# A latent-attention prologue with its key places one iteration sooner, its row roots earlier on GpSimd, and idle transposes ahead of its first products

## The reference, cut to what matters

```python
def mla_project(h, w_in, q_a_g, kv_a_g, w_uq, w_ukv, qk_g_q, qk_g_k, pos):
    c_q, c_kv, k_pe = jnp.split(h @ w_in, ODD_SPLIT, axis=-1)          # 512 | 256 | 64 columns
    q = to_heads(rms_norm(c_q, q_a_g) @ w_uq, MLA_HEADS)
    kv = to_heads(rms_norm(c_kv, kv_a_g) @ w_ukv, MLA_HEADS)
    ...
    q = rms_norm(q, qk_g_q); k = rms_norm(k, qk_g_k)                    # then rotary positions
```

## Time and profile before

| what | value |
|---|---|
| median of 3 runs | 3112.95 us (3111.66 to 3117.14) |
| the profiled execution's own time | 3118.48 us |
| its span in the trace | 3116.7 us |
| mean granted PE clock | 0.958 of full |
| PE busy / DVE busy / ACT busy / POOL busy | 91% / 68% / 50% / 23% of the span |
| prologue of the latent attention | about 1638.6 to 1812 us of the span |
| main part of the latent attention | about 1812 to 2375 us |

### The profile page before, as it was taken

The page is one execution under the profiler, slowest core; times in us unless marked ns, Lnnn a source line. Parts: engine busy times, 40 slices in busy tenths (PEclk is TensorE's granted clock), DMA queues, the critical chain, the costliest instruction groups (busy, mean ns, idle before and its releaser), DMA issues. The chain is left out here.

```text
span 3116.7 us, 47472 instructions
## 1 busy us (share of the span) xinstructions
PE 2840.2 (91%) x16808; PEld 2280.3 (73%) x16808; DVE 2119.9 (68%) x2536; ACT 1558.8 (50%) x2199; POOL 719.8 (23%) x1243
## 2 busy tenths in 40 slices
PE   6999998869489999999996879999998949999998
PEld 3766676758377777777766768888887838888887
DVE  3576762944666776777655457776765479999997
ACT  2312112532155555555544356766674227777775
POOL 0000000820011211211204665565620001111111
PEclk8999998989789999999998999999999969999999
DMA  6357734444548878878862000000013369999995
GB/s 226 117 208 241 250 115 172 147 177 144 209 180 296 298 292 295 298 294 293 298 234 86 18 9 16 25 16 20 8 66 112 129 268 381 400 396 384 400 400 187
DMA packets 129837, 631.41 MB, mean 203 GB/s; under 512 B 14913, under 2 KB 29377, under 8 KB 70946
## 3 DMA queue, kind: packets, MB, share of 16 engines
q1 hardware_dynamic: 117410, 591.86, 50.0%
q0 software_dynamic: 12288, 37.75, 4.8%
HBM read 563.40 MB, written 66.16 MB: 202 GB/s over the span
## 5 line engine op out<-in xcount | busy, mean ns | idle before, releaser
L1823 DVE TENSOR_TENSOR ex_wlo<-ring,ex_whi 128x2048 fp32r<-128x2048 f32 x384 | 877.4, 2290 | 213.2 <-ACT ex_whi L1752 208.5
L1752 ACT CAST ex_whi<-ring 128x2048 fp32r<-128x2048 f32 x384 | 727.5, 1904 | 295.1 <-PE psum L1717 210.8
L1717 PE MATMUL psum<-ex_whi,ex_xh 128*128 128x512 f32 x1024 | 403.8, 394 | 0.0
L1717 PE MATMUL psum<-ex_whi,ex_xl 128*128 128x512 f32 x1024 | 399.4, 390 | 0.0
L1717 PE MATMUL psum<-ex_wlo,ex_xh 128*128 128x512 f32 x1024 | 398.7, 389 | 0.0
L469 PE MATMUL psum<-fr_whi,fr_hh 128*128 128x512 f32 x560 | 223.9, 401 | 12.8 <-DVE fr_hl L653 11.4
L1717 PEld LDWEIGHTS psum<-ex_whi,ex_xh 128*128 128x128 f32 x1024 | 192.2, 188 | 45.1 <-issue 6.6
L1717 PEld LDWEIGHTS psum<-ex_whi,ex_xl 128*128 128x128 f32 x1024 | 192.2, 188 | 40.8
L1717 PEld LDWEIGHTS psum<-ex_wlo,ex_xh 128*128 128x128 f32 x1024 | 192.4, 188 | 38.6
L469 PE MATMUL psum<-fr_wlo,fr_hh 128*128 128x512 f32 x560 | 218.1, 391 | 0.7 <-DVE fr_wlo L659 0.7
L469 PE MATMUL psum<-fr_whi,fr_hl 128*128 128x512 f32 x560 | 218.2, 391 | 0.0
(11 more groups left out here) (305 smaller groups left out, 6021.7 us busy)
## 6 DMA issues: line engine op xcount, KB each, us to landing
ring<-in_moe_w SPq DMA_DIRECT2D x384, 1024.0 KB, 8.5
fr_raw<-in_mod_w SPq DMA_DIRECT2D x40, 1024.0 KB, 5.8
rec_d<-fr_work SPq DMA_DIRECT2D x72, 256.0 KB, 6.1
fr_raw<-in_ev_w_in SPq DMA_DIRECT2D x14, 1024.0 KB, 5.8
ring<-rec_d SPq DMA_DIRECT2D x10, 1024.0 KB, 15.3
h_d<-ring SPq DMA_DIRECT2D x18, 512.0 KB, 3.0
fr_arena<-in_mod_w SPq DMA_DIRECT2D x8, 1024.0 KB, 11.9
ring<-mod_d SPq DMA_DIRECT2D x15, 512.0 KB, 7.4
```

What stands on the lines that cost most here:

```text
L1717: last = nc.tensor.matmul(g.psum[:, 2 + i % 2, :], x[:, 4 * b + k, :], w[n][:, k, :], start=(b == 0 and k == 0 and first == 0), stop=(b == ...
L1752: nc.scalar.copy(whi[m % RING][:, :, :], slot(i)[:, 4 * b:4 * b + 4, :]).then_inc(hi_set, 1)
L1823: nc.vector.tensor_tensor(wlo[n][:, :, :], slot(i)[:, 4 * b:4 * b + 4, :], whi[n][:, :, :].bitcast(F32), ALU.subtract).then_inc(lo_set, 1)
```

## The change

In `Heads`, `first[p]` becomes a pair: the query place of tile `ORDER[p-2]` and the key place of tile `ORDER[p-1]`, either of which may be None. So the key place of a tile comes one iteration sooner, after the query place, while the sequence of place numbers stays as it was. On POOL `root(1)` comes ahead of the three `low_w`, and in the loop `root(p+3)` after `latent_root(p)` stands in for `root(p+2)` at the head. On ACT `square(1)` follows `square(0)` directly, ahead of the casts of blocks 2 to 7, and `high_up(0)`/`low_up(0)` (the key weight's high and low part) move from iteration 1 to iteration 0. On PE, 36 transposes of the identity into PSUM bank 7 stand ahead of `turn_h(0)`, behind a wait for the first weight cast, and 12 behind it; nobody reads them.

```diff
-        self.first = [[s for s, step in enumerate(self.steps) if p >= 2 and step[1:] == (0, self.ORDER[p - 2])]
-                      for p in range(NT + 2)]
+        at = {step[:1] + step[2:]: s for s, step in enumerate(self.steps) if step[1] == 0}
+        self.first = [(at.get(("q", self.ORDER[p - 2])) if p >= 2 else None,
+                       at.get(("k", self.ORDER[p - 1])) if 1 <= p <= NT else None) for p in range(NT + 2)]
...
 # TensorE
+                pe.wait_ge(wh_set, 1)
+                turn_idle(nc, g, 7, 36)
                 turn_h(0)
+                turn_idle(nc, g, 7, 12)
                 for p in range(NT + 2):
-                    places = hd.first[p]
+                    queries, keys = hd.first[p]
...
-                    if places:
-                        place(places[0])
+                    if queries is not None:
+                        place(queries)
                     if latent:
                         down(p, 3, QL, KVL + ROPE, latkv_out, kv_sum)
                     if p == 0:
                         turn_h(1)
-                    if len(places) > 1:
-                        place(places[1])
+                    if keys is not None:
+                        place(keys)
...
 # ScalarE
                 square(0)
+                square(1)
                 for k in range(2, 5):
                     high_w(k)
                 high_h(0)
                 for k in range(5, KD):
                     high_w(k)
-                square(1)
...
                     if p == 0:
                         high_h(1)
-                    if len(places) > 1:
-                        place(places[1])
-                    if p == 1:
                         high_up(0)
+                    if keys is not None:
+                        place(keys)
...
 # VectorE
-                    for s in places:
-                        take(s)
-                        low(s)
-                    if p == 1:
+                    if p == 0:
                         low_up(0)
+                    for s in hd.first[p]:
+                        if s is not None:
+                            take(s)
+                            low(s)
...
 # GpSimd
                 root(0)
+                root(1)
                 for k in range(5, KD):
                     low_w(k)
-                root(1)
                 root(2)
...
                 for p in range(NT + 2):
-                    places = hd.first[p]
-                    if 1 <= p < NT - 2:
-                        root(p + 2)
-                    if places:
-                        step(places[0])
+                    queries, keys = hd.first[p]
+                    if queries is not None:
+                        step(queries)
                     if p < NT:
                         latent_root(p)
-                    if len(places) > 1:
-                        step(places[1])
+                    if p < NT - 3:
+                        root(p + 3)
                     if p < NT:
                         base(p)
+                    if keys is not None:
+                        step(keys)
```

## The result

Over 8 runs each on the same chip, the changed kernel took 3105.74 us median (3099.71 to 3110.41) and the kernel before 3112.3 (3110.26 to 3117.14). The ratio is 0.9976, 95% interval 0.9966 to 0.9987: 7.5 us saved (4.0 to 10.6). Forecast were 7.7 us saved and 3105.2. The profiled execution took 3104.16 us, its span 3102.4.

The account below looks back on a forecast made before the run. PE was taken as the bound, with idle time and slow clock to win back in the prologue. 0.9 + 13.7 - 10.7 + 3.8 = 7.7 us saved, from the median 3112.95 to 3105.2; 8-in-10 range 3098.5 to 3111.5.

Parts of the forecast that it names:

- opening: First transposes and products on PE: idle transposes lift the clock, turn_h(0) takes 1.04 instead of 1.97 us; 0.9 us gained.
- roots: waits 7.7, slow clock 2.7: Prologue loop: row roots one tile ahead remove 7.7 us of PE waits for scaled rows and 2.7 of slow clock.
- latent waits under the key places: Prologue loop: key places an iteration sooner cover latent copies and norms, removing waits of 2.0 and 1.3 us.
- new waits and slow clock behind them: Iterations 2 and 4: PE newly waits for a key and for low_c, then runs slow; 10.7 us lost together.
- end: Last kv products to last tail place: 20.5 us instead of 25.8, less 1.5 for query place 5; 3.8 gained.
- rival A: New waits stay short (2.6 and 2.0 us) and PE keeps its clock: saving 13.8 us, 3099; chance 0.22.
- Key place 1: Iteration 2: PE waits 4.1 us for key step 0 on POOL (releaser L2652), with 2.2 us of slow clock behind.
- Key place 2: Iteration 4: PE waits 3.0 us for low_c(3), behind scale(6) on DVE, with 1.5 us of slow clock behind.
- margin of 2.2 us: Full iterations: POOL's key step ends at T+9.7, its transposing place stands at T+11.9, so 2.2 us to spare.
- rival C: POOL becomes the bound, as base and key step run beside scale in every iteration: slower, 3121 us; chance 0.05.
- Norm at +3.4, query 6 done by 5.8 to 6.5: End of the prologue: norm and query place 6, timed in us within the sum that gave 3.8 us gained.
- signs named for a right forecast: Profile marks, among them: new PE wait before key place 1, last kv products to first score product about 21 us, not 27.

Follow-up runs that it names:

- e11: The changed kernel run again, unedited but for the file; prologue 168.78 us, ratio 0.9973 to the kernel before.
- e1: The kernel before with only the new order of row roots (root(1), square(1), root(p+3)); prologue 162.46 us, ratio 0.9955 to the kernel before.
- e7: The changed kernel with more idle transposes in PE's waits (block 4, turn_h(2), iterations 2 and 4, the end); prologue 159.68 us, ratio 0.9951 to the kernel before.
- e3: The changed kernel without its 48 idle transposes; prologue 169.41 us, ratio 0.9988 to the kernel before.
- e5: The changed kernel with base(p) ahead of root(p+3) on POOL, the key step still behind the root; prologue 165.74 us, ratio 0.9981 to the kernel before.
- e8: The kernel before with only the new root order, plus idle transposes in the opening, ahead of turn_h(2) and at the end; prologue 157.78 us, median 3094.3 us.
- e4: The changed kernel with root(p+3) moved on POOL behind base(p) and the key step; prologue 174.97 us, ratio 1.0011 to the kernel before.
- e9: e8 with base(p) ahead of root(p+3) and of the query step on POOL; prologue 164.66 us, ratio 0.9967 to the kernel before.
- e6: The changed kernel with low_c(p-1) ahead of scale(p+2) on DVE; prologue 169.27 us, ratio 0.9985 to the kernel before.
- e10: The changed kernel with root(1) and square(1) back at their old places behind low_w and the casts; prologue 166.64 us, ratio 0.9979 to the kernel before.

## Why the prediction was right

The total was right within 0.2 us by the ratio, and that is partly luck: the interval is 4.0 to 10.6 us, and the same kernel gave 8.4 in e11. By the prologue, 5.4 us were saved where 7.7 were summed, and three errors of 2.7, 1.4 and 3.5 us stand behind that, the first against the other two. The terms:

| term | forecast | measured |
|---|---|---|
| opening | 0.9 gained | 0.5 lost (0.9 gained in four other runs, the tile's landing apart) |
| roots: waits 7.7, slow clock 2.7 | 10.4 gained | 10.2 gained (e1) |
| latent waits under the key places | 3.3 gained | 5.3 gained, as a remainder |
| new waits and slow clock behind them | 10.7 lost (its four parts add to 10.8) | 9.8 lost |
| end | 3.8 gained | 0.3 gained |

**Opening**, from the stage's start to the end of `turn_h(1)`: 26.27 us before, 26.80 after. The idle transposes did lift the clock (`turn_h(0)` in 1.09 us instead of 1.97), PE did wait for block 4, and block 4 came 0.9 us sooner, all as written. What failed is "full clock on the first twelve products gains nothing: it ends in a wait for block 4": I ended the reckoning at this wait and left out the clock behind it. PE fell to 1.2 GHz in the 1.74 us (in e11 just behind the wait), and the next twelve products took 4.52 us instead of 3.07. Against rival A's "the clock fell only some 2 us or more after PE went idle" stands this shorter wait. In four other runs with these idle transposes it did not fall, and there they gained the 0.9 that was summed.

**Roots.** L2447 waits 3.5 us for L2599 instead of 17.9, and no scaled tile behind the third is awaited. e1 shows it as the cause, and sizes it: from the end of `turn_h(1)` to the end of the last kv products went 120.2 us before and 109.9 in e1, 10.2 gained where 7.7 + 2.7 were summed. The changed kernel took 115.9, with query place 5 in it (1.5), so 5.7 gained net where 3.0 were summed. With 10.2 for the roots and 9.8 of new losses, 5.3 us remain for the waits that the key places were to cover, forecast at 3.3. They weren't measured by themselves, but the three waits that e1 still has there (0.93 and 1.42 us for norms, 1.78 for a scaled tile, 4.1 together) are all gone in the changed kernel.

**New waits.** Key place 1: forecast 4.1 us and 2.2 of slow clock, measured 4.31 and 1.5, with the releaser that was named. Key place 2: forecast 3.0 and 1.5, measured 2.41 and 1.6. (The slow clock is read against the same instructions at full clock, in e7 for the first and in e3 for the second.) base(1) beside the scale cost 1.7 us more (2 x 1.18 against 2 x 0.32), forecast 1.5. Here the port rule of the Trainium skill (SBUF — State Buffer, section "SBUF: two separate sides") had been weighed against the earlier trace rows and set at 1.5 us instead of the whole 2.5. The runs bear out both: e5's rows show the rule in full, each small POOL operation ending with the DVE operation beside it or up to 0.4 us later, and also that one slips in between the two (L2649 in 0.45 us), for which DVE pays (1.51 us for L2449 instead of 1.23). No iteration from the fifth to the ninth waited, so the margin of 2.2 us held, and rival C (POOL becomes the bound) fell.

**End.** From the end of the last kv products (1773.4) to the end of the second tail place (1797.4) went 24.0 us, forecast 20.5, before 25.8; with the 1.5 us of query place 5 moved to the front, 0.3 is gained and not 3.8. The step that failed is "Norm at +3.4, query 6 done by 5.8 to 6.5". The norm came at +4.2 (1777.60), and query place 6 ended at +8.2, since its products took 2.71 us at 1.2 GHz and not 1.47. The waits behind it were as forecast: query 7 began 4.6 us after query 6 ended (4.9), the second tail place 5.2 after query 7 ended (5.1). But query 7 too was slow, 2.77 us for its products, and so were the two tail places (2.47 and 2.51). I had taken half of the end slow, as before; all of these query places were, and only key place 7 ran at full clock. In e7, with PE kept busy there, the query places took 1.47 each. So of the signs named for a right forecast one failed: from the last kv products to the first score product went 25.9 us and not about 21.

**The range** of 3098.5 to 3111.5 held. Its rival A (waits short and clock kept, 3099) was not what this change did: its two new waits were 6.7 us. e7, in which the clock is kept though PE's work still waits, ran at 3096.2.

What stays open: 1.2 of the 5.3 us of the remainder; what decides whether the clock falls at the 1.74 us wait, and with it whether the 14 transposes ahead of block 4 are needed to hold it (without them it held in four of six); and whether other fillings of PE's waits do better than those of e8, which were not tuned.

## What to carry to other kernels

Before you move work ahead in a full queue, follow the instruction that needs the result as well as the one that makes it: the wait left POOL and came back on DVE (e4), at full length. Where two parts of a change touch one chain, run each alone: here one part gained 11.6 us, and the other took 6.9 of it back while the sum still looked like a success. And price a wait of PE with the clock behind it: transposes that nobody reads took 7 to 9 us off this prologue, more than the waits that the change added. They must fit their wait, though: where PE came to them at 1.2 GHz they held real work back (e9).

## What the runs showed of the hardware

**The same wait does not always cost the clock.** Six kernels had the same work ahead of block 4 and the same idle time of 1.73 to 1.75 us. In two (after, e11) PE then ran mostly at 1.2 GHz, 4.52 and 4.61 us for twelve products; in four (e4, e5, e6, e10) it stayed at 2.4 GHz, 3.07 us. The idle time ahead of `turn_h(0)` does not tell the two kinds apart: it was 2.69 and 2.32 us in the first, 2.72 in e4 and 1.2 to 1.6 in the other three. Nor is block 4 the only such place: behind the wait of iteration 4 the eight transposes took 1.91 us in the changed kernel (2.41 us waited) and 1.04 in e3 (2.42 us waited). A single profile can differ by 1.5 us for this at each such place; two kernels should be compared from the place behind it on.

**A small POOL operation waits as long as a large one.** L2647 and L2651 work on 128x1 elements, 0.27 and 0.56 us alone. Beside a 1.3 to 1.5 us DVE operation they took 1.34 and 1.53 (e5), and L2672 in e9 1.44. The Trainium skill (SBUF — State Buffer, section "SBUF: two separate sides") has the loser "fully block", which these rows agree with. That it holds for one element per partition too I had not counted in what I expected of e5.

**It works the other way too.** The scale beside POOL's `low_w` took 2.98 us in the changed kernel; in e10, which moves it out from beside `low_w`, it took 1.28. So semaphores are not all that ties DVE and POOL together in time.
